# The rows' dot products read their second operand from PSUM instead of SBUF

## The reference

```python
u = peer_u[idx]                                              # (n, 8, 16, 1024)
a = gelu(einsum('nd,nhkd->nhk', xb, u))                      # xb: the tokens' normed rows
v = peer_v[idx]
return einsum('nhk,nhkd->nd', g * a, v)                      # g: softmax over the chosen scores
...
hp = hp + peer_ffn(rms_norm(hp, g_ffn), w_pq, sub_keys, peer_u, peer_v)
```

## Time and profile before

| | |
|---|---|
| time, median of 3 runs | 2325.94 us (2323.11 to 2328.35) |
| profiled execution: its time, its span | 2343.9 us, 2341.9 us |
| busy: PE, DVE, POOL, ACT | 1517.6, 1393.7, 1213.6, 199.0 us |
| TensorE's granted clock over the span | 0.806 of full speed |
| moved by DMA | 726.18 MB, mean 310 GB/s |
| gathers from peer_u on POOL | 520, mean 1211 ns |
| gathers from peer_v on POOL | 520, mean 952 ns |
| U products on DVE (L1238) | 512, mean 1225 ns |

### The profile page before, as it was taken

One profiled execution on the slowest core, in us unless ns is written; L12 is line 12 of the kernel. 1 busy time (PEld: TensorE's weight loads), 2 busy tenths in 40 slices (PEclk: granted clock), 3 DMA queues, 4 the chain that ended last, 5 costly groups with the idle time before them and its releaser, 6 DMA issues.

```text
span 2341.9 us, 17442 instructions
## 1 busy us (share of the span) xinstructions
PE 1517.6 (65%) x6048; PEld 667.2 (28%) x6048; DVE 1393.7 (60%) x3124; ACT 199.0 (8%) x440; POOL 1213.6 (52%) x1126
## 2 busy tenths in 40 slices
PE   6999498987664925888991003994005999000998
PEld 3444243554632512233551001221001222000222
DVE  2878942361877776411589889965988304788000
ACT  3124200012001101001100000000000000100000
POOL 0311202100126866333344777777777776877774
PEclk9999698969876956799996556997557997555999
DMA  7786538564548988977774999999999999899998
GB/s 265 278 303 217 186 139 329 188 230 162 189 143 339 335 329 310 393 274 278 273 296 130 337 364 385 409 409 393 398 360 382 409 409 358 313 371 378 400 409 334
DMA packets 208423, 726.18 MB, mean 310 GB/s; under 512 B 20192, under 2 KB 25056, under 8 KB 197968
## 3 DMA queue, kind: packets, MB, share of 16 engines
q0 software_dynamic: 160368, 616.91, 69.3%
q1 hardware_dynamic: 39776, 99.22, 11.4%
q10 hardware_dynamic: 8192, 8.95, 1.1%
HBM read 714.96 MB, written 10.04 MB: 310 GB/s over the span
## 4 chain that ended last, share of the span: by engine, by line
PE 48%; POOL 25%; DVE 10%; issue 8%; DMA 6%; ACT 2%; SPq 0%; ACTq 0%; POOLq 0%; DVEq 0%
POOL arena L594 25%; PE ps L1787 20%; PE ps L1570 15%; PE ps L1947 3%; DVE arena L925 3%; DMA arena<-in_peer_v,arena 3%; DMA arena<-in_peer_u,arena 2%; DVE arena L1238 1%; DMA arena<-in_cache_diff_v,arena 1%; PE ps L1531 1%; PE ps L1965 1%; PE ps L1677 1%; PE ps L1853 1%; ACT ps L636 1%; PE ps L1743 1%
## 5 line engine op out<-in xcount | busy, mean ns | idle before, releaser
L594 POOL DMA_INDIRECT arena<-in_peer_u,arena x520 | 629.5, 1211 | 425.7 <-issue 153.3
L1238 DVE CUSTOM_DVE_ANT_0 arena<-arena 128x1024 f32<-128x1024 f32 x512 | 618.1, 1225 | 105.1 <-DMA arena<-in_peer_u,arena 95.5
L594 POOL DMA_INDIRECT arena<-in_peer_v,arena x520 | 495.2, 952 | 285.2 <-PE ps L1787 167.7
L1787 PE MATMUL ps<-arena 128*32 128x512 f32 x2048 | 589.0, 619 | 8.8 <-DMA arena<-in_peer_v,arena 7.0
L1570 PE MATMUL ps<-arena 128*128 128x512 f32 x960 | 434.3, 608 | 7.9 <-ACT arena L646 5.1
L1778 PE MATMUL ps<-arena 128*128 128x128 f32 x4 | 1.9, 474 | 541.6 <-DVE arena L925 541.6
L1787 PEld LDWEIGHTS ps<-arena 128*32 128x32 f32 x2048 | 166.3, 112 | 425.6 <-issue 307.7
L1570 PEld LDWEIGHTS ps<-arena 128*128 128x128 f32 x960 | 182.7, 194 | 238.1 <-issue 229.9
L925 DVE TENSOR_TENSOR arena<-arena,ps 128x512 f32<-128x512 f32 (+6 forms) x59 | 48.9, 830 | 291.6 <-PE ps L1787 165.8
L925 DVE TENSOR_TENSOR arena<-arena 128x256 f32<-128x256 f32 (+7 forms) x339 | 196.9, 608 | 21.1 <-DMA arena<-in_state_ret 6.7
L1778 PEld LDWEIGHTS ps<-arena 128*128 128x128 f32 x4 | 0.7, 182 | 544.6 <-DVE arena L925 544.6
(11 more groups left out here) (228 smaller groups left out, 1281.7 us busy)
## 6 DMA issues: line engine op xcount, KB each, us to landing
arena<-in_w_pq SPq DMA_DIRECT2D x8, 2048.0 KB, 15.2
arena<-in_w_in SPq DMA_DIRECT2D x7, 2048.0 KB, 10.8
arena<-in_peer_u,arena POOLq DMA_INDIRECT x520, 6.3
arena<-in_peer_v,arena POOLq DMA_INDIRECT x520, 8.8
arena<-in_w_out SPq DMA_DIRECT2D x4, 2048.0 KB, 8.6
arena<-in_w_mq SPq DMA_DIRECT2D x4, 2048.0 KB, 13.4
arena<-in_w_mo SPq DMA_DIRECT2D x4, 2048.0 KB, 14.0
arena<-in_cache_mem_k SPq DMA_DIRECT2D x8, 1024.0 KB, 8.0
```

Source lines behind the costliest of these rows:

```text
L594: return pool.indirect_dma_start(slot, None, table[0], bass.IndirectOffsetOnAxis(idx.bitcast(U32), 0))
L1238: dve.tensor_tensor_reduce(row, row, QR[:, b, :], 1.0, 0.0, ALU.mult, ALU.add, DOTS[:, k:k + 1]).then_inc(s["u_used"], 1)
L1787: last = pe.matmul(PS[32 * j:32 * j + 32, 6 + half, :], window(n, i, j), row[:, 512 * half:512 * half + 512], start=(n == 0 and i == 0), s ...
```

## The change

Each block's normed rows are copied by ACT from `QR` to two banks of PSUM (block 0: banks 6 and 7; block 1: 0 and 1; blocks 2 and 3: 2 and 3), once for each block, and the U products read them there. DVE's products wait for the copy by a new semaphore, `x_in_ps`. The copies stand in ACT's list at three places: at the head of group 1 (block 0), behind the last router scores (blocks 1 and 2), and ahead of the sample's gelu (block 3). PE waits for the end of block 2's products before all of the sample's rows that it writes to banks 0 to 3, where it waited from the third on. Two pairs of semaphores are merged into one each, with the same meeting points.

```diff
+        X_BANKS = {0: 6, 1: 0, 2: 2, NBLK - 1: 2}
+
+        def x_copy(b):
+
+            return PS[:, X_BANKS[b]:X_BANKS[b] + 2, :].rearrange("p a c -> p (a c)")
...
+            def x_to_ps(b):
+                act.copy(x_copy(b), QR[:, b, :]).then_inc(s["x_in_ps"], 1)
...
             for g, blocks in enumerate(GROUPS):
                 prompt = [b for b in blocks if b != SMP]
+                if g:
+                    act.wait_ge(s["xn_ready"], TURN + 2 * len(GROUPS[0]))
+                    act.wait_ge(s["idxt_ready"], 1)
+                    act.wait_ge(s["mixed_done"], NB - len(GROUPS[0]))
+                    x_to_ps(0)
...
+            act.wait_ge(s["rs_taken"], 2 * NSUB)
+            act.wait_ge(s["smp_scores_taken"], NSUB)
+            x_to_ps(1)
+            x_to_ps(2)
             gate_exp(1)
...
             act.wait_ge(s["u_used"], used_through("u", SMP))
+            x_to_ps(NBLK - 1)
             act.activation(sgl, sdot, ACT.Gelu).then_inc(s["gelu_done"], 1)
...
             def dot_products(b, k0, k1):
+                dve.wait_ge(s["x_in_ps"], b + 1)
 
                 for k in range(k0, k1):
                     row = row_landed(dve, "u", b, k)
-                    dve.tensor_tensor_reduce(row, row, QR[:, b, :], 1.0, 0.0, ALU.mult, ALU.add,
+                    dve.tensor_tensor_reduce(row, row, x_copy(b), 1.0, 0.0, ALU.mult, ALU.add,
                                              DOTS[:, k:k + 1]).then_inc(s["u_used"], 1)
...
                     for k in range(DB):
-                        if k >= 2:
-                            pe.wait_ge(s["u_used"], used_through("u", 2) + k - 1)
+                        pe.wait_ge(s["u_used"], used_through("u", 2) + max(k - 1, 0))
```

More of the change, by code:

```diff
@@ L256 @@
         line_stored toe_loaded past_ps past_ready kvidx_ready rows_turned rowsT_done scores_ready sc_biased
[L257 to L265, removed]
@@ L266 @@
-        slot_in2 slot_in3 slot_in4 slot_in5 slot_in6 slot_in7 slot_in8 slot_in9 slot_in10 slot_in11 slot_in12
-        slot_in13 slot_in14 slot_in15 slot_in16 qdec_loaded sq_stored qb_in0 qb_in1 mixed_turned mixed_done
-        tile_in3""".split()
+        nmax_ready exp_done w_ready wmat_turned wT_ready av_done dif_taken srow_saved s_scored colmax_turned
+        maxbc_ready sexp_done esum_ready z_ready coef_ready pv_done om_ready dif_row_ready rqd_ready ret_scores
+        ret_sc_ready ret_out ret_state ret_rows rqm_ready kexp_ready outer_ready ns_ready ns_stored0 ns_stored1
@@ new lines @@
+        ns_stored2 state_stored hsq_ready hrstd_done mix_ready x_again done_stored final_ready mkr_loaded
+        mkr_turned mkT_done mv_loaded cs_ready cmax_ready cexp_done ce_turned ceT_ready co_ready co_taken
+        cqb_ready cs_scored ccolmax_turned cmaxbc_ready csexp_done cesum_ready cz_ready ccoef_ready cpv_done
+        com_ready crow_ready sk_loaded sk_turned skT_done rqp_ready rqp_taken rs_ready rs_taken xb_ready
+        gelu_done weight_ready y_ready u_used v_used select_steps picked idx_turned idxt_ready gate_arg
@@ L271, in build @@
+        gate_exp_done gates_done w_turned wx_ready slot_in0 slot_in1 slot_in2 slot_in3 slot_in4 slot_in5 slot_in6
+        slot_in7 slot_in8 slot_in9 slot_in10 slot_in11 slot_in12 slot_in13 slot_in14 slot_in15 slot_in16
+        qdec_loaded sq_stored qb_in0 qb_in1 mixed_turned mixed_done tile_in3 largest_ready clargest_ready x_in_ps""".split()
 def build(nc, x_prompt, x_sample, mem_prompt, cache_diff_k, cache_diff_v, page_table, state_ret, cache_mem_k,
@@ L1090, in _ @@
             tt(colmax[0:DB, :].rearrange("p (b c) -> p b c", b=DB), colmax[0:DB, :].rearrange("p (b c) -> p b c", b=DB),
-               sself_m[0:DB], ALU.max).then_inc(s["colmax_ready"], 1)
+               sself_m[0:DB], ALU.max).then_inc(s["largest_ready"], 1)
             dve.wait_ge(s["new_kv_stored"], 16 * NSTORES)
@@ L1097, in _ @@
             link(dve.tensor_reduce(mcol[0:64, :], PS[0:64, 6, 0:P], AX.X, ALU.max))
-            dve.tensor_scalar(mdiag[0:64, :], ident[0:64, 0:64], mcol[0:64, :], None, ALU.mult).then_inc(s["maxdiag_ready"], 1)
+            dve.tensor_scalar(mdiag[0:64, :], ident[0:64, 0:64], mcol[0:64, :], None, ALU.mult).then_inc(s["largest_ready"], 1)
             turned_row("rq", 1, DV, 0)
@@ L1399, in _ @@
                     dve.tensor_reduce(ccol.rearrange("p (b h) -> p b h", b=DB), CS4.rearrange("p b j h -> p b h j"), AX.X, ALU.max
-                                      ).then_inc(s["ccolmax_ready"], 1)
+                                      ).then_inc(s["clargest_ready"], 1)
                     dve.wait_ge(s["ccolmax_turned"], 1)
                     link(dve.tensor_reduce(cmx[0:32, :], PS[0:32, 4, 0:P], AX.X, ALU.max))
-                    dve.tensor_scalar(cmd[0:32, :], ident[0:32, 0:32], cmx[0:32, :], None, ALU.mult).then_inc(s["cmaxdiag_ready"], 1)
+                    dve.tensor_scalar(cmd[0:32, :], ident[0:32, 0:32], cmx[0:32, :], None, ALU.mult).then_inc(s["clargest_ready"], 1)
                     dve.wait_ge(s["cmaxbc_ready"], 1)
@@ L1648, in largest @@
                 if i == 0:
-                    pe.wait_ge(s["colmax_ready"], 1)
+                    pe.wait_ge(s["largest_ready"], 1)
                     pe.transpose(PS[0:64, 6, 0:P], colmax, ident).then_inc(s["colmax_turned"], 1)
                 if i == 1:
-                    pe.wait_ge(s["maxdiag_ready"], 1)
+                    pe.wait_ge(s["largest_ready"], 2)
                     pe.matmul(PS[:, 7, 0:64], ones[0:64, :], mdiag[0:64, :], start=True, stop=True).then_inc(s["maxbc_ready"], 1)
@@ L1868, in _ @@
                         expert_step(g, ("mk", b))
-                    pe.wait_ge(s["ccolmax_ready"], 1)
+                    pe.wait_ge(s["clargest_ready"], 1)
                     pe.transpose(PS[0:32, 4, 0:P], ccol, ident).then_inc(s["ccolmax_turned"], 1)
-                    pe.wait_ge(s["cmaxdiag_ready"], 1)
+                    pe.wait_ge(s["clargest_ready"], 2)
                     pe.matmul(PS[:, 5, 0:32], ones[0:32, :], cmd[0:32, :], start=True, stop=True).then_inc(s["cmaxbc_ready"], 1)
```

## The result

The changed kernel takes **2267.53 us** (median of 4 runs, 2259.87 to 2271.76) against 2327.14 for the kernel before (4 runs): ratio 0.9723, 95% interval 0.9659 to 0.9787. Measured once more it is 2262.93 us against 2331.15 (6 and 11 runs), 0.9717 with 0.9681 to 0.9754. The ratios are reckoned from the single runs and are not quotients of these medians. So it is faster by some 60 to 68 us; the forecast was 2237 us, 89 us faster, and 2205 to 2280 its range. The profiled execution took 2264.58 us with a span of 2262.8; that of before had 2341.9, 79.1 more.

What follows compares the result with a forecast made beforehand. POOL's gathers, held by products with two SBUF inputs, were taken to pace the U stretches. Gains of 31.0 + 11.6 + 27.5 + 19 = 89.1 us off 2325.94 gave 2237 us, range 2205 to 2280.

Steps and rivals of the forecast that it cites:

- The mechanism: U stretches: a product with both inputs in SBUF holds gathers; one input in PSUM frees them, 0.93 us each; chance 0.80.
- the slower rival: U products: reading PSUM costs more in an unbroken run, 1.72 us apart, +150 us, 2476; chance 0.04.
- the upper bound, 2278: Whole kernel: block 0 gives nothing and rows come at 1.344 us, 22 us less gain.
- the prediction's second rival: U stretches: the transfers hold them anyway, only gapless runs gain, 26 us in all, 2300; chance 0.08.
- Block 1: Block 1's products: with gathers freed they end at 1408.1 instead of 1439.08, 31.0 us less.
- the sum's second figure: Block 1's end: DVE alone would need until 1406.5, beside 1408.1 by the transfers.
- Block 2: Block 2's products: rows at 1.28 us from the 11th on, end at 1770.0 instead of 1781.63, 11.6 us less.
- Block 0: Group 1: DVE's 33.9 us of waits for u rows shrink by 5, 11 and 3, 19 us less.
- Block 3: Block 3's products: end at 2139.0 instead of 2166.53, late gelu included, 27.5 us less.
- the late gelu: Sample before block 3: copy of 1.03 and table load of 1.28 make the gelu 2.3 us late.
- From 1989.3 on 116 more rows take 148.5 us: Block 3 from its 12th product: remaining rows follow at the transfers' pace, 1.28 us each, ending at 2139.0 with the product.
- The base: Whole kernel: 89.1 us taken off the runs' median 2325.94, not the profiled 2343.9, the 0.8% between counted as under one us.

Runs made afterwards that it cites:

- the first two experiments: Against the changed kernel: all U products read SBUF again, 2339.14 us; blocks 1 and 2 read both inputs from SBUF and write product rows to PSUM, 2295.02 us.
- the halved rows: Changed kernel with block 2's u-row gathers from the 18th on fetching 512 in place of 1024 numbers: 2246.78 us, ratio to the kernel before 0.9632.
- the version with both changes: Changed kernel with the sample's v-row gathers set among block 3's u rows and block 3's copy ahead of the sample wait: 2253.58 us, ratio to before 0.9685.

## Why the prediction was right, and where 30 us went

The mechanism held at each of its places: gathers of 0.94 us beside products of 1.22, block 2 at 410 GB/s, products 1.14 us apart with their rows landed (so PSUM costs nothing in an unbroken run, and the slower rival is dead), and shown by undoing the operand alone. One step of it was too small: a gather can lose more than a product's length (6.55 us in the last section). That the time lies inside the range is in part luck: the upper bound, 2278, allowed for a block 0 that gives nothing and for rows at 1.344 us, and neither came true; the two misses below, of block 3 and of the base, were not allowed for.

The Trainium skill, SBUF — State Buffer, section Who interferes with whom, says that a DVE instruction with two SBUF inputs contends with a GpSimd instruction that reads SBUF; the first two experiments agree (in block 1 maxima of 1992 and 2007 ns with two, 942 with one). Its inference, that a two-input elementwise operation does not hold up descriptors, is not tested here by itself: the gathers also read their row numbers from SBUF, and what is held may be this read. The 358 GB/s of the prediction's second rival (the Trainium skill, SBUF — State Buffer, section A bandwidth-pool intuition that's wrong (but worth ruling out)) are, in the row that they come from, a stack's bandwidth divided by two cores. One core runs here, so the measured 409 does not speak against that figure, as the prediction had it.

- **Block 1**, 31.0 forecast, 28.4 in the pair of profiles. The bound changed hands as in the sum's second figure: the products run at 1.14 us until 29 are left and at 1.28 from there, so both limits are nearly one.
- **Block 2**, 11.6 forecast, 9.8 measured; the halved rows show the transfers to be the limit.
- **Block 0**, 19 forecast, 22.1 measured, and the nearness is partly luck: the term was made of DVE's waits for u rows alone, and these fell by 12.2, from the 33.9 of the earlier trace rows to 21.7. From the first to the last product of block 0 the time fell by 13.9 us (234.6 to 220.7); the other 8.2 lie behind, up to block 1's first product (345.2 to 337.0), where the forecast had nothing. There TensorE was busy 289.4 us for 297.3, and in the first 81 to 85 us of it its granted clock was 0.85 for 0.77; why was not tested. The waits that are left:

```profile
DVE arena L1257 <- DMA arena<-in_peer_u,arena: 6.8, 10, 0.8
...
DVE arena L1257 <- DMA arena<-in_peer_u,arena: 14.7, 17, 2.5
...
DVE arena L1257 <- DMA arena<-in_peer_u,arena: 0.2, 1, 0.2
```

- **Block 3**, 27.5 forecast with the late gelu in it, 19.0 measured. The step that was mis-sized: "From 1989.3 on 116 more rows take 148.5 us". The gelu was late as said (2.60 us of DVE's wait, the copy and the table load of 1.02 and 1.28), but the rows did not follow at 1.28 us from the 12th on. The 12th to 19th products came 1.27 to 2.27 us apart, since the slots of their rows were waited for on TensorE, and from the 12th to the end it took 158 us, where 150 were forecast. A wait for TensorE was there before, too, but shorter (4.1 us), as the gathers were held. With the rows later and the copy early the stretch is 188.3, 27.4 less than before; the forecast's 27.5 still had the late gelu in it.
- **The base**, the larger part. The step: "It lies 18 us above the median of the runs, 0.8%, which on 89 us is less than one; so 2325.94 - 89.1". Taken off the profile's own time, the same sum gives 2254.8, 9.8 under the changed kernel's profile of 2264.58, and of this difference block 3 is 8.5. So of the 30 us, 18 are the base, 10 the sum, and 3 lie between the changed kernel's profile and its median. What the profile of before has above the median is not spread evenly: between two profiles 13 us apart, block 1's products differ by 16, through the held gathers, which are just what the change removes. But block 1 can't be the whole of it. With only block 0 on PSUM, the rest of the change is worth as much in the medians (55 to 59 us) as in the profiles (55.5); what falls short is block 0's step, 6.7 us in the medians.
- **What stays open in the base.** What a run at the median of before looks like inside was not seen, and where its shorter time comes from stays open. So does whether being profiled makes such a kernel slower: five profiles of five lie above the medians, while the two of the changed kernel and the one with only block 0 on PSUM lie within 3 us of theirs. Nor was the spread known when the prediction took 0.2% for it, from three runs within 5 us: of 41 timed runs of before, 39 lie between 2314.7 and 2349.7, two above. The longer ones tend to have the lower granted clock over the span (2343.08 us at 0.807, 2315.60 at 0.812). That may follow from longer U stretches, in which the clock is 0.50, or add to the time; no run separates the two.

## What to carry to other kernels

When a GpSimd instruction that should have one length shows two (0.94 and 1.99 us here), look at where in a VectorE instruction it starts, and if that one has two inputs in SBUF, try one of them in PSUM; the test is to undo that one operand. Before taking a hold away, walk the slots in turn behind it and ask whose release comes next: the sample's rows cost some 8 us that nobody saw while the gathers were slow anyway; a later place in the order gave 5 to 6 of them back, and with the copy ahead of the wait about all. And take a sum off the time of the execution that it was read from; the distance to the median may lie in the very stalls that the change removes.

## What the runs showed of the hardware that was not expected

- Two SBUF inputs hold a gather only by where it starts. In the kernel before most of block 1's gathers are short (median 996 ns in the earlier trace rows), and which are long differs from run to run (medians of 975 to 1212). The timelines show what decides. Three gathers at the start of block 3's products begin 0.59, 0.33 and 0.05 us into a product and last 1.44, 1.70 and 1.99 us, so that each ends 0.81 to 0.82 us behind the end of that product. The last gather shown was held through five products in a row, and again ends 0.81 us behind the fifth:

```profile
1977.02 1.22 DVE L1238 CUSTOM_DVE_ANT_0 arena<-arena 128x1024 f32<-128x1024 f32 x1
1979.31 1.22 DVE L1238 CUSTOM_DVE_ANT_0 arena<-arena 128x1024 f32<-128x1024 f32 x1
1981.60 1.22 DVE L1238 CUSTOM_DVE_ANT_0 arena<-arena 128x1024 f32<-128x1024 f32 x1
...
1977.61 1.44 POOL L594 DMA_INDIRECT arena<-in_peer_u,arena  x1 [3.47 <-PE ps L1973]
1979.64 1.70 POOL L594 DMA_INDIRECT arena<-in_peer_u,arena  x1 [0.60 <-PE ps L1973]
1981.65 1.99 POOL L594 DMA_INDIRECT arena<-in_peer_u,arena  x1 [0.30 <-issue]
...
2023.93 6.55 POOL L594 DMA_INDIRECT arena<-in_peer_u,arena  x1 [0.30 <-issue]
```

Counted over the four profiles of before: 618 gathers begin 0.06 to 1.0 us into a product or a scalar_tensor_tensor of 128x1024 with two SBUF inputs, and 614 of them end 0.81 to 0.83 us behind its end; the other four were held through more than one. Of 956 that begin later in it none lasts over 1.04 us, though 868 of them run on into the next one: a gather that has begun is not held any more. Those that begin within the first 0.06 us go either way, and why some are held through several instructions stays open. In the changed kernel 372 gathers begin 0.06 to 1.0 us into a product, and all last 0.93 to 0.95.

- The scalar_tensor_tensor of the final norm, four in a row with two inputs in SBUF, do the same. In the changed kernel's second profile a gather begins 0.96 us into the first and lasts 1.14 us; in the version with both changes one begins 0.15 us into one of them and lasts 1.95.

```profile
1999.86 4.89 DVE L952 SCALAR_TENSOR_TENSOR arena<-arena 128x1024 f32<-128x1024 f32 x4 [0.28 <-ACT arena L646]
...
2000.82 1.14 POOL L599 DMA_INDIRECT arena<-in_peer_u,arena  x1 [0.30 <-issue]
```

- The change made the kernel steadier: 39 of 41 timed runs of before lie between 2314.7 and 2349.7 us, the ten of the changed kernel between 2259.0 and 2271.8.
